# A six-layer model on one core: four heads of values first in the gated-delta projection, and five smaller moves in the order of work

## The reference, cut to what matters

```python
for i in range(4):                       # first block: gdn, hgrn, gla, gdn
    x = layer_norm(DN_ALPHA * x + mixer_i(x), ...)
    x = layer_norm(DN_ALPHA * x + swiglu(x, ffn_w_in[i], ffn_w_down[i]), ...)
for l in range(2):                       # second block: two "four" layers
    x = x + mixed(rms_norm(x)) @ w_out[l]
    x = x + conv_swiglu(rms_norm(x))

# gated_deltanet (gdn), up to the recurrence
p = x @ w_in                             # [256, 4112]
qkv, z, b, a = split(p)                  # q, k, v: 8 heads x 128 each; z 1024; b, a: 8 each
qkv = silu(causal_depthwise_conv(qkv, conv_w))     # 4 taps along the tokens
q, k = l2_normalize(q), l2_normalize(k)
beta, g = sigmoid(b), -exp(a_log) * softplus(a + dt_bias)
```

## Time and profile before

| | |
|---|---|
| three executions | 2189.66, 2189.79, 2190.99 us; median 2189.79 |
| profiled execution | 2192.47 us by its own time, 2190.8 us span |
| PE busy | 2120.5 us, 97% of the span |
| DVE, ACT, POOL busy | 1488.6, 880.3, 181.4 us |
| mean DMA | 152 GB/s, 333.80 MB |

### The profile page before, as it was taken

How to read it: one execution, slowest core, us unless ns; L and a number is a source line. 1 busy time by engine, 2 the same in 40 slices (tenths; PEclk the granted TensorE clock), 3 DMA queues, 4 the chain that set the end, 5 groups by cost and what they waited for, 6 DMA issues and landing times.

```text
span 2190.8 us, 35328 instructions
## 1 busy us (share of the span) xinstructions
PE 2120.5 (97%) x14257; PEld 1844.5 (84%) x14257; DVE 1488.6 (68%) x1963; ACT 880.3 (40%) x1121; POOL 181.4 (8%) x150
## 2 busy tenths in 40 slices
PE   8999999999999999999899999998989999989999
PEld 7988888799788888888799888887768998768998
DVE  5957755777844558844586685446587887478887
ACT  2244444331444413444414344445554334654332
POOL 4721000000000000000064300000100000100000
PEclk9999999999999999999999999999999999999999
DMA  7511655552465553555555037554325555314552
GB/s 221 174 59 60 204 184 188 174 168 82 160 197 184 171 175 105 186 187 191 155 158 167 6 99 238 186 181 131 116 68 183 183 183 171 120 65 141 187 192 96
DMA packets 265605, 333.80 MB, mean 152 GB/s; under 512 B 16493, under 2 KB 228594, under 8 KB 265474
## 3 DMA queue, kind: packets, MB, share of 16 engines
q1 hardware_dynamic: 265473, 331.93, 47.0%
HBM read 330.84 MB, written 1.05 MB: 151 GB/s over the span
## 4 chain that ended last, share of the span: by engine, by line
PE 88%; DVE 8%; ACT 2%; issue 2%; POOL 0%; DVEq 0%; POOLq 0%; ACTq 0%
PE bank L564 45%; PE bank L532 30%; PE bank L1015 2%; DVE w_lo L2077 1%; PE bank L1070 1%; PE bank L615 1%; PE bank L785 1%; PE bank L877 1%; PE bank L941 1%; DVE sq L2041 1%; ACT stat L1487 1%; PE bank L891 1%; DVE w_hi L2075 1%; ACT w_hi L1533 1%; DVE xt L2041 1%
## 5 line engine op out<-in xcount | busy, mean ns | idle before, releaser
L2077 DVE TENSOR_TENSOR w_lo<-ring,w_hi 128x2048 fp32r<-128x2048 f32 (+2 forms) x293 | 620.6, 2120 | 381.5 <-ACT w_hi L1533 379.0
L1533 ACT ACTIVATE w_hi<-ring 128x2048 fp32r<-128x2048 f32 (+2 forms) x222 | 419.3, 1890 | 492.3 <-PE bank L564 291.3
L564 PE MATMUL bank<-w_lo,xh 128*128 128x512 f32 x992 | 268.1, 393 | 0.0
L532 PE MATMUL bank<-xh,w_hi 128*128 128x256 f32 (+2 forms) x1816 | 250.6, 292 | 11.7 <-DVE w_hi L2075 11.2
L532 PEld LDWEIGHTS bank<-xh,w_hi 128*128 128x128 f32 (+2 forms) x1816 | 234.2, 195 | 24.6 <-issue 16.6
L564 PE MATMUL bank<-w_hi,xh 128*128 128x512 f32 x896 | 243.1, 393 | 6.2 <-ACT xh L1487 3.1
L532 PE MATMUL bank<-xh,w_lo 128*128 128x256 f32 (+3 forms) x1880 | 245.2, 283 | 0.0
L564 PE MATMUL bank<-w_hi,xl 128*128 128x512 f32 x896 | 241.2, 391 | 0.7 <-DVE xl L2031 0.7
L532 PE MATMUL bank<-xl,w_hi 128*128 128x256 f32 (+2 forms) x1816 | 238.9, 285 | 0.0
L532 PEld LDWEIGHTS bank<-xh,w_lo 128*128 128x128 f32 (+3 forms) x1880 | 231.9, 188 | 2.2 <-issue 0.2
L532 PEld LDWEIGHTS bank<-xl,w_hi 128*128 128x128 f32 (+2 forms) x1816 | 227.7, 192 | 0.7
(11 more groups left out here) (320 smaller groups left out, 2428.7 us busy)
## 6 DMA issues: line engine op xcount, KB each, us to landing
ring<-in_ffn_w_in_dram SPq DMA_DIRECT2D x264, 512.0 KB, 4.4
ring<-in_ffn_w_down_dram SPq DMA_DIRECT2D x88, 512.0 KB, 4.2
ring<-in_gdn_w_in_dram SPq DMA_DIRECT2D x64, 512.0 KB, 5.1
ring<-in_ffn_w_out_dram SPq DMA_DIRECT2D x44, 512.0 KB, 4.0
ring<-in_w_in_dram SPq DMA_DIRECT2D x36, 512.0 KB, 4.7
ring<-in_hgrn_w_in_dram SPq DMA_DIRECT2D x32, 512.0 KB, 4.5
ring<-in_gla_w_in_dram SPq DMA_DIRECT2D x24, 512.0 KB, 4.6
ring<-in_gdn_w_out_dram SPq DMA_DIRECT2D x16, 512.0 KB, 4.4
```

The source lines that it names most:

```text
L532: m = nc.tensor.matmul(cols, *((wk, xk) if tokens == ALL else (xk, wk)), start=(first and step == 0 and k == 0 and (j % 2 == 0)), stop=(la ...
L564: m = nc.tensor.matmul(bank[:, 0:width], xin[:, k0 + k, rows_of], w[:, k, c * width:(c + 1) * width], start=(first and step == 0 and k == ...
L1533: nc.scalar.activation(high_part(u)[:, 0:n], ring[:, u % RING, 0:n], ACT.Copy).then_inc(*act_hi.tick())
L2077: v.tensor_tensor(w_lo[:, u % RING, 0:share], w[:, 0:share], high[:, 0:share], ALU.subtract).then_inc(*dve_lo.tick())
```

## The change

1. gdn's projection (layers 0 and 3) begins with a "tok" pair: the values of heads 0 to 3 with tokens stationary. Then comes `ba`, then the eight q, k units, two v units (heads 4 to 7) and the gate. There are 17 units as before. ACT copies the pair to `vb`; after `ba`, PE transposes it back in eight 128x128 transposes (`v_to_channels`) into two newly claimed banks; DVE convolves these behind its own units in turns 4 and 5, and releases the banks there.
2. `params_to_columns` on PE moves from after unit 2 to after unit 4; `decay_rows` and ACT's part of the parameters move from turn 0 to turn 2, `setup` from turn 1 to turn 3.
3. The layer norm ahead of a gdn layer makes the low part of x for t = 0 where hgrn and gla do, before the second half is normalised.
4. At the start of the kernel, `xh`, `xl` and the weight parts are made alternately.
5. hgrn: ACT's `exp logits` moves from `gla_decays` (after the last f unit) to behind the second f unit. gla: the first batch of DVE splits grows from 6 to 8.
6. "four": ACT makes `high` of mixers 0 and 1 ahead of `rstd` of mixer 3; a DVE `split` moves ahead of the wait for mixer 3; nine `stay_awake` matmuls on bank 3 stand ahead of the claims of `out_project`.

```diff
-FILL = {"mixed": 9, "gdn": 5, "c2": 7, "kbeta": 5, "masked": 4, "softmax": 2}
+FILL = {"out": 9, "mixed": 9, "gdn": 5, "c2": 7, "kbeta": 5, "masked": 4, "softmax": 2}
...
-N_QK, N_CONV = 8, 12
+N_QK, N_CONV = 10, 12
...
-        u = [(4096, 16, "pair8", "ba", 0)]
-        u += [(256 * i, 256, "cm", "conv", 2 * i) for i in range(12)]
+        u = [(2048, 256, how, "v", 0) for how in ("tok0", "tok1")]
+        u += [(4096, 16, "pair8", "ba", 0)]
+        u += [(256 * i, 256, "cm", "conv", 2 * i) for i in (0, 1, 2, 3, 4, 5, 6, 7, 10, 11)]
...
-                            second = [psum.claim(pe, "proj", layer, 2, t) for t in range(2)] if kind != "four" else [None]
+                            second = [psum.claim(pe, "proj", layer, 2, t) for t in range(2)] if kind in ("hgrn", "gla") else [None]
...
-                    if layer == 0 and n == 2:
+                    if kind == "gdn" and n == 2:
+                        v_to_channels(layer)
+                    if layer == 0 and n == 4:
                         params_to_columns()
...
+            def v_to_channels(layer):
+                pe.wait_ge(*act_proj.at("v", layer, 0))
+                for i in range(2):
+                    b = psum.claim(pe, "proj", layer, "v", i)
+                    for j in range(2):
+                        for t in range(2):
+                            c = (2 * i + j) * P
+                            m = nc.tensor.transpose(b[:, j * T + t * HALF:j * T + (t + 1) * HALF], vb[:, t, c:c + P], ident[:, :])
+                    m.then_inc(*pe_gdn.tick("v T", layer, i))
...
+                if CHAIN[layer][0] == "four":
+                    stay_awake(FILL["out"], 3)
...
# ACT: project
+                        if n in (4, 5):
+                            act.wait_ge(*dve_conv.at("conv", layer, n + 4))
+                            run(s, pj2(8 + 2 * n), pj2(8 + 2 * n), ACT.Silu, "conv", layer, n + 4)
...
+                        if idx == 2:
+                            act.wait_ge(*dve_gla.at("logits", layer))
+                            run(act_gla, flat(lbs[:, 0:4]), flat(lbs[:, 0:4]), ACT.Exp, "exp logits", layer)
...
-                    if layer == 0 and n == 0:
+                    if layer == 0 and n == 2:
                         params_to_columns()
-                    if kind == "gdn" and n == 0:
+                    if kind == "gdn" and n == 2:
...
# ACT: four
-                    if n:
-                        high(order[n - 1])
+                    if n == 1:
+                        high(order[0])
+                        high(order[1])
+                high(order[2])
                 high(order[3])
...
# DVE: project
-                    if kind == "gdn" and n == 0:
+                    if kind == "gdn" and n == 2:
...
-                    if layer == 0 and n == 1:
+                    if layer == 0 and n == 3:
                         setup()
...
+                    convolved(idx, "proj", layer, n)
+                    if kind == "gdn" and n in (4, 5):
+                        dve.wait_ge(*pe_gdn.at("v T", layer, n - 4))
+                        convolved(8 + 2 * n, "proj", layer, "v", n - 4)
...
# DVE: layer_norm
-                elif not all_at_once:
+                else:
                     low_rows(n, 0, 0)
                     low_rows(n, 0, 1)
...
-                due(5 if kind == "hgrn" else 6)
+                due(5 if kind == "hgrn" else 8)
...
# DVE: four
                 log_weights(3)
+                split()
                 dve.wait_ge(*pe_four.at("o", layer, 3))
...
                 tt(s, oc4[:, 3, :], oc4[:, 3, :], pj2(16), ALU.mult, "gated", layer)
-                split()
...
# DVE: start (ACT likewise, with rows_high and cast)
-            for t in range(2):
-                for c in range(2):
-                    low_rows(-1, t, c)
-            split(HI)
+            low_rows(-1, 0, 0)
+            split()
+            low_rows(-1, 0, 1)
+            split()
+            low_rows(-1, 1, 0)
+            low_rows(-1, 1, 1)
+            split(HI - 2)
```

More of the change, by code:

```diff
@@ L1907, in gla_decays @@
                 if kind == "hgrn":
-                    act.wait_ge(*dve_gla.at("logits", layer))
-                    run(s, flat(lbs[:, 0:4]), flat(lbs[:, 0:4]), ACT.Exp, "exp logits", layer)
                     act.wait_ge(*dve_gla.at("bounds", layer))
@@ L1995, in four @@
                          "rstd", layer, m)
-                    if n:
-                        high(order[n - 1])
+                    if n == 1:
+                        high(order[0])
+                        high(order[1])
+                high(order[2])
                 high(order[3])
-            for t in range(2):
-                for c in range(2):
-                    rows_high(-1, t, c)
-            cast(HI)
+            rows_high(-1, 0, 0)
+            cast()
+            rows_high(-1, 0, 1)
+            cast()
+            rows_high(-1, 1, 0)
+            rows_high(-1, 1, 1)
+            cast(HI - 2)
             act.wait_ge(*pool_setup.at("constants"))
@@ L2150, in project, with convolved @@
                     dve.wait_ge(*pe_unit.at("unit", layer, n))
-                    b = psum.bank("proj", layer, n)
-                    conv(dve_conv, [pj[:, base + idx + j, :] for j in range(2)], [b[:, j * T:(j + 1) * T] for j in range(2)],
-                         lambda j, tap: par(tiles + tap * n_tiles + idx + j), 4, ("conv", layer, idx // 2))
-                    psum.release(dve_conv, "proj", layer, n)
+                    def convolved(idx, *key):
+                        b = psum.bank(*key)
+                        conv(dve_conv, [pj[:, base + idx + j, :] for j in range(2)], [b[:, j * T:(j + 1) * T] for j in range(2)],
+                             lambda j, tap: par(tiles + tap * n_tiles + idx + j), 4, ("conv", layer, idx // 2))
+                        psum.release(dve_conv, *key)
+                    convolved(idx, "proj", layer, n)
+                    if kind == "gdn" and n in (4, 5):
+                        dve.wait_ge(*pe_gdn.at("v T", layer, n - 4))
+                        convolved(8 + 2 * n, "proj", layer, "v", n - 4)
                     if kind == "four":
@@ L2298, in layer_norm @@
                     split(2)
-                to_rms, all_at_once = next_kind == "four", next_kind == "gdn"
+                to_rms = next_kind == "four"
                 chunk(0, 0)
@@ L2321, in layer_norm @@
                     gained_rows(n + 1, 1)
-                elif all_at_once:
-                    low_rows(n, 0, 0)
-                    low_rows(n, 0, 1)
                 last = n + 1 if to_rms else n
```

## The result

The changed kernel takes 2208.86 us (median of 4 runs, 2203.66 to 2210.55) against 2190.39 us of the kernel before on the same chip (2189.66 to 2192.24): a ratio of 1.0079, interval 1.0067 to 1.0091. It is 18.5 us slower by the medians; the ratio, which is of means, makes it 17.3. The forecast was 2199.4, slower by 9.6, and its range ended at 2205: the direction was right, the size about half, and the result lies above the range.

The account below looks back on a forecast made before the run. PE was taken to bound the kernel (97% busy, 88% of the chain). Layer 0 +17.9, layer 3 -5.5, hgrn -6.5, gla -5.0 and fillers +8.7 sum to +9.6 us: 2199.4 us, range 2187 to 2205.

Parts of the forecast that it names:

- `setup` 1.6: Layer 0, DVE's turn 3: setup was priced at 1.6 us from rows of the profile before.
- unit 9 at 53 and 56: Layer 3: unit 9's high part ready at 53 us, due at 56, so PE doesn't wait.
- Layer 0, +17.9: Layer 0's projection: PE waits for banks held by v until DVE's convolutions release them; +17.9 us, opening included.
- The opening: Layer 0's start: parameters transposed at 44.25, 14.5 us later with 11.5 us more done, so 3.0 us lost.
- half clock: Layer 0's start: the first pair's four high products were taken to run at half the full clock.
- Y + 24.2: Layer 0: unit 6 gets its bank 24.2 us after Y, the start of the parameter transposes; PE stands 17.2 us.
- Layer 3, -5.5: Entry into layer 3's projection: PE reaches unit 3 in 21.6 us against 27.4, without later waits; -5.5 us taken.
- hgrn -6.5 and gla -5.0: Projections of hgrn and gla: earlier casts remove PE's waits of 3.77 and 3.50 us and slow stretches after; -6.5, -5.0.
- The fillers, +4.35 each: Ahead of out_project in both "four" layers: fillers wait for bank 3, then delay ready products; +4.35 us a layer.
- Rival A: Layer 0: v's banks don't hold PE, only casts do; 10.2 us sooner, 2189.2, no change; chance 0.12.
- Rival B: "four" layers: filler runs in the wait, bank 3 being free; -3.2 us a layer, 2184.3; chance 0.09.
- Rival C: Layer 3's double turns stall PE as in layer 0, or hgrn and gla get half; +6, 2205; chance 0.12.

Follow-up runs that it names:

- v_later: The changed kernel with v's transposes issued two units later in layer 0, behind the parameters' transposes: 2197.62 us, 1.0025 of the kernel before.
- dve_lows: The changed kernel with the low parts of units 5 and 6 (layer 0) and 3 to 5 (layer 3) wholly on DVE: 2202.01 us, ratio 1.0050.
- hgrn_gla_only: The kernel before with only hgrn's earlier exponentials on ACT and gla's first batch of eight weight splits: 2180.4 us, ratio 0.9951.
- filler_in_gap: The changed kernel with the nine matmuls ahead of the output projection on bank 0 instead of bank 3: 2198.21 us, 1.0034 of the kernel before.
- setup_early: The changed kernel with DVE's setup at turn 1 of layer 0 instead of turn 3: 2203.32 us, 1.0053 of the kernel before.
- no_filler: The changed kernel without the nine matmuls ahead of the output projection in layers 4 and 5: 2197.88 us, 1.0033 of the kernel before.

## Why the prediction was half right

The sum was +9.6 us, the profiled executions differ by 15.4 and the medians by 18.5. The waits, and what ends them, were right in layer 0, in hgrn and gla and ahead of the fillers. The step that failed is a price: DVE's operations were walked at the durations that they have with POOL idle. In layer 0 "`setup` 1.6" took 4.9 us, and in layer 3 "unit 9 at 53 and 56" came to 57.7 and 56.7, so that PE waits there where I had said that it doesn't. Two stretches had no term at all (+2.3 us together), and 3.0 us lie between the traces and the medians.

- **Layer 0, +17.9 forecast, +19.8 measured.** The mechanism is as written: the claim order, the idle time, its releaser L2067 and the two units that wait. `v_later` shows that the order of claims carries 10.1 us. The opening was 1.05 us better than walked (43.20 for 44.25), and 0.25 came back after unit 7. The "half clock" of its first products was an estimate from durations: the four took 2.08 us, as such rows take at 0.50 granted (2.05 at 1623.63), but no window of either trace from 8 to 16 us shows a clock under 1.00. Against that, "`setup` 1.6" of turn 3 took 4.9, since its first cast was held 3.2 us by POOL. I took its price from rows of before in which POOL had no work beside it, though the `rows` of 1.73 us in layer 3 of before showed what POOL does. Unit 6 came at Y + 27.4 in place of Y + 24.2, after 20.54 us of idle time where I had written 15 to 19. (Y of before is 29.83 in the earlier trace rows, not 29.7; it moves the terms by 0.1.) In the six traces with the old layer 0 unit 13 ends at 98.2 to 100.4, in the four with the changed one and nothing moved at 120.1 to 120.2: the profiled pair gives the lower end of this loss, up to 22 us.
- **Layer 3, -5.5 forecast, -3.2 measured.** PE reaches unit 3 after 21.9 us; the walk said 21.6, though its parts as written add up to 22.25. The step "unit 8 at 44 ... unit 9 at 53 and 56" takes casts at 1.25 us where POOL is beside them. Two casts and `rows` were held, and DVE left `decay_rows` at 1128.95, 3.2 us later than in `dve_lows` (1124.00 in a layer that starts 1.8 us sooner). Counted from the last product (1095.57), the high part of unit 8 was there at 48.8, in time, and that of unit 9 at 57.7, when PE had stood for it from 56.7. Giving POOL's share to DVE brought 1.7 of the missing 2.3; 0.6 is that the feed-forward before it ended later.
- **hgrn -6.5 and gla -5.0:** -6.6 and -5.2, and the same with only these edits made.
- **The fillers, +4.35 each:** +5.2 and +3.2 in the profiled pair. Over the traces the stretch from layer 4's start to its feed-forward takes 168.3 to 172.9 us in the five kernels with the filler behind the bank (middle one 171.1) and 166.5 to 168.4 in the six with none (middle 166.7): +4.4. The next stretch, to layer 5's feed-forward, takes 351.7 against 347.5: +4.2. Together 8.6 for 8.7 forecast. By timing it is about 10. The number fits by luck, since two errors cancel. From layer 4's start the output projection begins 7.1 us later than before and not 4.35: the filler began 1.4 us later than walked, and took 5.59 us (0.31 an instruction, at 0.75 and 0.82 granted) where I had 3.9 (0.217, from a stretch of before with 1.00 granted; "2 x 256 columns" was an estimate, for which the rows have only that 24 products of 512 columns take 5.47 us, 0.228 each). And I gave nothing for the clock that the products then find at 1.00 (before, 0.50 and 0.78 in their first two windows of 4 us): its 96 products take 22.2 us in place of 24.9, and from its start to the first product behind the next norm it is 26.98 in place of 29.26. In layer 5 it is 5.4 us later, and 26.54 for 27.88.
- **What no term had:** +1.3 us in layer 0's mixer. From the filler behind unit 16 to the output projection it takes 78.2 to 79.2 us in all eight traces with the new layer 0, and 76.7 to 77.7 in the six with the old one. 0.8 of it is the round of banks again, at a place that the diff doesn't touch. The source gives the banks when the claims are counted: the second of two `u1` had bank 2 before, and has bank 4 now, since the projection makes other claims ahead of it. `psum.next = 4` then hands the first `o` bank 4 in both kernels, and now this claim waits for ACT's copy of the second `u1`. The first product of `o`, before and after:

```profile
191.15 0.67 PE L882 MATMUL bank<-mats,ct 128*128 128x256 f32 x2
```

```profile
212.21 0.70 PE L899 MATMUL bank<-mats,ct 128*128 128x256 f32 x2 [0.69 <-ACT ct L1504]
```

This 0.69 is there in all eight traces with the new layer 0 and in none of the six with the old; in layer 3, where the second `u1` of the changed kernel has bank 1, it is in none. The other 0.5 us build up in the levels before, where DVE and PE alternate, and +1.0 us lie between layer 3's unit 13 and layer 4. I made no run for either; their cause is open.
- **From traces to medians, 3.0 us.** The forecast put its 9.6 us on the median of before. The profiled execution of before was 2.1 us slower than the median of the comparison, and that of the changed kernel 0.9 faster than its own. Layer 0's opening is one source of the first: unit 13 ended at 98.3 in `hgrn_gla_only`, whose layer 0 is that of before, for 100.3, and all the difference is in the first products (144 matmuls in 17.23 us for 19.34). The runs of the five kernels with the filler behind the bank spread over 4.9 to 7.6 us, those of the other changed ones over 1.9 to 4.9; that the filler causes it isn't shown.

Rival A, that v's banks don't hold PE, is refuted by `v_later`. Rival B, the filler in the wait, didn't happen, and `filler_in_gap` shows that it would have cost some 5 us less a layer than what happened, but gained nothing over leaving it out: the 2 us of clock that I gave it are taken back by DVE. Rival C's stall in layer 3 is there in small, 1.15 us, but by way of held casts and not of v's banks.

Layer 0 (19.8, bound 20) and the fillers (8.6, bound 12) stayed inside their own bounds, so the range fell short by what had none. Its terms were walks over durations of DVE rows of before. The hold by POOL, 3.2 us in layer 0 and 1.7 in layer 3, is one effect that worked in one direction; the mixers' 2.3 us had no term, and no bound was given for how far one profiled execution lies from the median. Even the sum of all upper bounds that were given, 20 and 12 with the rest as forecast, is 2204.8.

## What to carry to other kernels

Before a new claim goes into a round of banks, walk the round to whoever gets that bank next and ask what must have released it: here an order of two calls was worth 10 us. And walk it on to the next place where the round is set to a fixed bank: two claims more or less ahead of it decide who is met there. Filler matmuls want a bank that is free when the wait begins: in bank 0 the nine ran for 4.05 us inside PE's idle time, in bank 3 for 5.59 us behind 3.34 us of it. Even then they gained nothing here (2198.21 against 2197.88), since what followed the products waited for DVE. When a diff moves DVE work, look which POOL operations it will then stand beside, and don't price it by a row that stood alone (0.15 us for a cast that took 3.38 beside POOL).

## What the runs showed of the hardware

A running POOL subtraction of two tiles in SBUF (4.0 us) held a DVE cast or tensor-scalar that reads and writes SBUF until it ended: an 8x8 cast took 3.38 us for 0.15, an 8x256 tensor-scalar 3.60 for 0.34, a 128x2048 cast 3.18 for 1.22. Small ones were held as large ones, for 3.23, 3.26 and 1.96 us; with POOL's operation gone they took 0.15, 0.33 and 1.22 again (`dve_lows`). The hold shows as a longer duration and not as idle time in brackets (the row of 3.38 has none). So these two engines met outside the semaphores, which the section on the chip gives as the only place. The convolution's tensor-scalars and its steps, which read from a bank, weren't held: of the 56 tensor-scalars in the changed kernel's trace 42 begin while such a POOL subtraction runs, of the 168 steps 116, and each takes 0.47 to 0.49 us. In `setup_early` POOL and DVE run side by side:

```profile
58.06 3.93 POOL L1471 TENSOR_TENSOR w_lo<-ring,w_hi 128x1536 fp32r<-128x1536 f32 x1 [1.44 <-DVE w_hi L2101]
```

```profile
58.62 0.87 DVE L2061 TENSOR_SCALAR pj<-bank,params 128x256 f32<-128x256 f32 x2
59.53 2.68 DVE L2067 SCALAR_TENSOR_TENSOR pj<-bank,params,pj 128x255 f32<-128x255 f32 x6
```

Both take what they take everywhere else in these traces. By what the one kind is held and the other not, no run here shows.

Second, the granted clock's fall after idle time cost nothing that the time shows at the place where it was feared: with a mean of 1.00 throughout the start of layer 4's projection (`filler_in_gap`) and of 0.71 and 0.86 in two windows of 4 us of it (`no_filler`) the medians are 2198.21 and 2197.88.
